# The last expert's down weights in idle up buffers, a rebuilt routing chain and a rebuilt end in a one-core decoder block

## The reference

```python
xn = rms_norm(h, norm_ffn)
logits = xn @ w_router + b_router
top_logit, top_e = lax.top_k(logits, 4)
top_w = softmax(top_logit)
# for each expert e, over the tokens that chose it:
hb = xn[tok] @ w1[e] + b1[e]                       # 1024 -> 2048
ob = clamped_swiglu(hb) @ w2[e] + b2[e]            # 1024 -> 1024
h = h + sum over the four experts of top_w * ob
out = rms_norm(h, norm_final)[:, 16:]
```

## Time and profile before

| | |
|---|---|
| three runs | 1355.83, 1360.45, 1358.1 us, median 1358.1 |
| profiled execution | 1358.35 us, its span 1356.6 us, mean granted clock 0.997 |
| PE busy | 1304.2 us (96%) |
| DVE, ACT, POOL busy | 459.3 (34%), 320.4 (24%), 66.7 (5%) |
| DMA | 461.85 MB, mean 340 GB/s |
| chain that ended last | PE 61%, DMA 29%, issue 4%, POOL 3%, DVE 2%, ACT 1% |

### The profile page before, as it was taken

The page is one execution under the profiler, slowest core; times in us unless marked ns, Lnnn a source line. Parts: engine busy times, 40 slices in busy tenths (PEclk is TensorE's granted clock), DMA queues, the critical chain, the costliest instruction groups (busy, mean ns, idle before and its releaser), DMA issues.

```text
span 1356.6 us, 17927 instructions
## 1 busy us (share of the span) xinstructions
PE 1304.2 (96%) x7105; PEld 638.0 (47%) x7105; DVE 459.3 (34%) x1129; ACT 320.4 (24%) x649; POOL 66.7 (5%) x74
## 2 busy tenths in 40 slices
PE   7999999999999999999999999999999999999995
PEld 5858888899974333333333322333333333333331
DVE  4838889988534211112111211111121111211111
ACT  3636767755411111011101101100110010111011
POOL 0000004422103000000000000000000000000000
PEclk9999999999999999999999999999999999999998
DMA  6431334244878999999999999999999999999994
GB/s 238 148 124 64 125 125 168 107 162 187 337 289 323 422 403 426 429 428 430 427 430 427 429 429 428 429 427 430 428 429 429 428 386 424 431 427 429 428 426 164
DMA packets 33763, 461.85 MB, mean 340 GB/s; under 512 B 3808, under 2 KB 3808, under 8 KB 5552
## 3 DMA queue, kind: packets, MB, share of 16 engines
q1 hardware_dynamic: 33424, 460.63, 81.5%
q10 hardware_dynamic: 288, 0.52, 0.1%
HBM read 460.09 MB, written 1.05 MB: 340 GB/s over the span
## 4 chain that ended last, share of the span: by engine, by line
PE 61%; DMA 29%; issue 4%; POOL 3%; DVE 2%; ACT 1%; SPq 0%; POOLq 0%; DVEq 0%; ACTq 0%
PE bank L1348 58%; DMA ring<-wts_dram 29%; POOL work L517 1%; POOL work L514 1%; PE bank L1690 1%; PE bank L1696 1%; DMA ring<-slabs_dram 1%; DVE split L913 0%; PE bank L1712 0%; PE bank L1479 0%; DVE work L847 0%; DVE work L846 0%; DVE work L845 0%; ACT split L559 0%; PE bank L1499 0%
## 5 line engine op out<-in xcount | busy, mean ns | idle before, releaser
L1348 PE MATMUL bank<-ring,work 128*64 128x512 f32 (+5 forms) x2248 | 541.7, 592 | 29.1 <-DMA ring<-wts_dram 28.1
L1348 PE MATMUL bank<-work 128*64 128x512 f32 (+8 forms) x2216 | 434.0, 546 | 3.2 <-DVE work L1267 1.0
L1348 PEld LDWEIGHTS bank<-ring,work 128*64 128x64 f32 (+2 forms) x2248 | 179.1, 142 | 340.4 <-issue 292.9
L1348 PEld LDWEIGHTS bank<-work 128*64 128x64 f32 (+4 forms) x2216 | 146.5, 143 | 258.8 <-issue 246.8
L1348 PE MATMUL bank<-hn_hi,split 128*128 128x256 f32 (+1 forms) x896 | 173.0, 288 | 1.4 <-DVE split L913 1.3
L1296 DVE COPY work<-bank 128x256 f32<-128x256 f32 x31 | 13.2, 425 | 473.8 <-PE bank L1712 473.8
L1348 PEld LDWEIGHTS bank<-hn_hi,split 128*128 128x128 f32 x896 | 141.4, 189 | 3.4 <-issue 1.9
L1348 PE MATMUL bank<-hn_lo,split 128*128 128x256 f32 (+1 forms) x448 | 127.2, 284 | 0.0
L1271 DVE TENSOR_SCALAR work<-bank 128x512 f32<-128x512 f32 x32 | 22.1, 692 | 273.4 <-PE bank L1348 273.4
L913 DVE TENSOR_TENSOR split<-ring,split 128x1024 fp32r<-128x1024 f32 x80 | 100.0, 1253 | 27.1 <-ACT split L559 26.8
L756 ACT ACTIVATE work<-bank 128x512 f32<-128x512 f32 x32 | 19.1, 598 | 328.3 <-PE bank L1348 324.2
(11 more groups left out here) (247 smaller groups left out, 899.9 us busy)
## 6 DMA issues: line engine op xcount, KB each, us to landing
ring<-wts_dram SPq DMA_DIRECT2D x127, 2048.0 KB, 24.2
work<-wts_dram SPq DMA_DIRECT2D x64, 2048.0 KB, 25.3
ring<-slabs_dram SPq DMA_DIRECT2D x23, 2048.0 KB, 7.5
ring<-slabs_dram SPq DMA_DIRECT2D x2, 1152.0 KB, 5.2
work<-wts_dram SPq DMA_DIRECT2D x2, 1024.0 KB, 19.8
work<-x_dram SPq DMA_DIRECT2D x3, 512.0 KB, 11.5
ring<-slabs_dram SPq DMA_DIRECT2D x1, 1536.0 KB, 12.0
ring<-slabs_dram SPq DMA_DIRECT2D x1, 1280.0 KB, 8.7
```

The source lines that it names most:

```text
L1348: return pe.matmul(o, lhsT, rhs, start=start, stop=stop)
```

## The change

Three parts, which touch one another only through the order of the work.

The last expert's down weights. Up buffers 0 and 1 of the even set take them (expert 30, the last even one, has used them after the second and the fourth k step of its up), the second in parts of 2048, 1024 and 1024 columns with a semaphore each. In SyncE's list they stand behind the second half of expert 30's.

```diff
             load_down(E - 2, E - 2)
-            load_down(E - 1, E - 1)
+            sp.wait_ge(up_used, (E - 2) * (W1_UNITS - 1) + 1)
+            sp.dma_start(w1_sb[0], unit_of(E - 1, W1_UNITS)).then_inc(w1_in[0], 16)
+            sp.wait_ge(up_used, (E - 2) * (W1_UNITS - 1) + 2)
+            for at, n, arrival in ((0, 2048, w1_in[1]), (2048, 1024, extra_in[0]), (3072, 1024, extra_in[1])):
+                sp.dma_start(w1_sb[1][:, at:at + n], unit_of(E - 1, W1_UNITS + 1)[:, at:at + n]).then_inc(arrival, 16)
...
+                if final:
+                    halves = [w1_sb[0][:, 0:UNIT // 2], w1_sb[0][:, UNIT // 2:UNIT], w1_sb[1][:, 0:UNIT // 2], w1_sb[1][:, UNIT // 2:UNIT]]
...
-                    if between is not None and k == 4:
+                    if between is not None and k == (2 if to == 4 else 4):
                         between()
```

```diff
-                link(d.max_index(idx[:, 8 * b:8 * b + 8], mx8[:, b, :], lg[:, b, :]))
-                link(d.tensor_copy(idxf[:, b, :], idx[:, 8 * b:8 * b + 8]))
-                link(d.tensor_tensor(chosen[:, b, :, :], iota_e[:, :].unsqueeze(1).to_broadcast([P, TOPK, E]),
-                                     idxf[:, b, 0:TOPK].unsqueeze(2).to_broadcast([P, TOPK, E]), ALU.is_equal))
-                d.tensor_reduce(mask[:, b, :], chosen[:, b, :, :].rearrange("p j e -> p e j"), AX.X, ALU.add).then_inc(mask_ready, 1)
+                link(d.memset(mx8[:, b, TOPK:8], -NEG))
+                link(d.match_replace(out=rest[:, b, :], in_to_replace=mx8[:, b, :], in_values=lg[:, b, :], imm_value=NEG))
+                d.tensor_scalar(mask[:, b, :], rest[:, b, :], NEG, None, ALU.is_equal).then_inc(mask_ready, 1)
...
+            a.activation(root, ssh4[:, 1, 1:2], ACT.Sqrt, scale=1.0 / D, bias=ssh[:, 1:2]).then_inc(root_ready, 1)
             xn_copy(1, 1)
...
+            def gather_first():
+                pe.wait_ge(hot_ready, 1)
+                for half, done in ((0, low_gathered), (1, gather_done)):
+                    for j in range(4):
+                        k = 4 * half + j
+                        for b in range(2):
+                            last = mm(bank[7 - half][:, j * SLOTS:(j + 1) * SLOTS], xn[:, b, k * P:(k + 1) * P], hot[:, b, :], b == 0, b == 1)
+                    last.then_inc(done, 1)
```

```diff
-            for b, n in ((1, 0), (1, 1), (0, 0)):
...
-            link(d.tensor_tensor(ssh[:, :], ssh4[:, :, 0], ssh4[:, :, 1], ALU.add))
-            rstd(rsh, ssh, D, EPS, rsh_ready)
+            d.tensor_copy(h2_copy, bank[1][:, :]).then_inc(h2_copied, 1)
+            d.wait_ge(h2_copied, 1)
+            d.tensor_tensor_reduce(out=hsq_end[:, 0, 512:D], in0=h2_copy, in1=bank[1][:, :], scale=1.0, scalar=0.0,
+                                   op0=ALU.mult, op1=ALU.add, accum_out=ssh4[:, 0, 1:2]).then_inc(h2_dve_squared, 1)
+            d.wait_ge(h2_squared, 1)
+            d.tensor_tensor(fin[:, 0, 0:512], bank[0][:, :], nfin[0][:, :], ALU.mult).then_inc(h2_scaled, 1)
...
+            link(d.reciprocal(y, root2))
+            link(d.tensor_tensor(tmp, y, y, ALU.mult))
+            link(d.scalar_tensor_tensor(tmp, ms2, -0.5, tmp, ALU.mult, ALU.mult))
+            d.scalar_tensor_tensor(y, tmp, 1.5, y, ALU.add, ALU.mult).then_inc(rsh_ready, 1)
```

More of the change, by code:

```diff
@@ L464, in _ @@
             with sp.If(cm > SLOTS):
+                sp.wait_ge(down_done, E)
                 with sp.Fori(1, SEQ // SLOTS) as r:
@@ L750, in _ @@
             top_weights(0)
+            a.activation(root, ones[:, 0:1], ACT.Sqrt).then_inc(root_table, 1)
             square_half(1, 1)
+            a.wait_ge(root_table, 1)
+            a.wait_ge(h1_squared, 4)
+            a.wait_ge(half_ready, 2)
+            a.activation(root, ssh4[:, 1, 1:2], ACT.Sqrt, scale=1.0 / D, bias=ssh[:, 1:2]).then_inc(root_ready, 1)
             xn_copy(1, 1)
@@ L789, in step @@
                     ob_of(t)
-                gathered(t0 + 1)
-                gatheredT(t0 + 1)
+                if r is FIRST:
+                    for half, done, ready in ((0, low_gathered, xgT_low_ready), (1, gather_done, xgT_ready)):
+                        cols = slice(half * SLOTS, (half + 1) * SLOTS)
+                        a.wait_ge(done, 1)
+                        a.activation(xgT[:, :, cols], bank[7 - half][:, 0:4 * SLOTS].rearrange("p (j t) -> p j t", j=4), ACT.Copy).then_inc(ready, 1)
+                else:
+                    gathered(t0 + 1)
+                    gatheredT(t0 + 1)
                 gathered(t0 + 2)
@@ L1738, in up, with down @@
                 last.then_inc(up_done, 1)
-            def down(t, to=6, actT=actT, between=None, first=None):
+            def down(t, to=6, actT=actT, between=None, first=None, later=False, final=False):
                 halves = [w2_sb[0][:, 0:UNIT // 2], w2_sb[0][:, UNIT // 2:UNIT], w2_sb[1][:, 0:UNIT // 2], w2_sb[1][:, UNIT // 2:UNIT]]
@@ L1785, in step @@
                     up_bias(t + 1)
-                    up(t + 1, pair, odd, between)
+                    up(t + 1, pair, odd, between, later=r is not FIRST)
                     if gathers:
@@ L1791, in step @@
                     if gathers:
-                        down(t, first=first)
+                        down(t, first=first, later=r is not FIRST)
                     else:
                         pe.wait_ge(scat_ready, t + 1)
-                        down(t, between=lambda: last_transposes(t + 1))
+                        down(t, between=lambda: last_transposes(t + 1), later=r is not FIRST)
                 def first_between(k):
+                    if r is FIRST and k == 4:
+                        counts()
+                    if r is FIRST and k == 2:
+                        pe.wait_ge(bias_in, 64)
+                        up_bias(t0, False)
                     if k == 6:
@@ L1829, in expert_round @@
                 if r is FIRST:
+                    pe.wait_ge(count_ready, 1)
                     cm.append(pe.value_load(cmax_i[0:1, 0:1], min_val=0, max_val=SEQ))
                 pe.wait_ge(up_read, t0 + E)
-                down(t0 + E - 1, 4, actT_last, lambda: scatter(t0 + E - 2))
+                down(t0 + E - 1, 4, actT_last, lambda: scatter(t0 + E - 2), later=r is not FIRST, final=r is FIRST)
+                pe.wait_ge(scat_ready, t0 + E)
+                scatter_last(t0 + E - 1)
             FIRST = 0
-            pe.wait_ge(xn_scaled, 2)
+            pe.wait_ge(xn_ready, 4)
             cm = []
```

210 lines of the change are left out of this document (123 added, 87 removed).

## The result

The changed kernel takes 1351.44 us (median of 5 runs, 1350.9 to 1353.01), the kernel before 1358.1 (5 runs, the three above and two more, 1355.83 to 1360.45): a ratio of 0.995, with an interval from 0.9937 to 0.9962. It is faster by 0.4 to 0.6%. The prediction was 1350.6. Its profiled execution is the one of 1351.44 us; its span is 1349.6 us, against 1356.6 before, 7.0 less.

A forecast was written before the change was run, and what follows sets the result against it. First experts were taken as bound by TensorE, later ones by the weight stream at 428 GB/s. Gains of 1.2 + 4.1 + 2.2 = 7.5 us took the median from 1358.1 to 1350.6 us, range 1347.9 to 1354.6.

The forecast's parts named there:

- Routing: Routing chain to the end of up(0): earlier masks and gather, less bias and counts inside up(0); 1.2 us gained.
- The last down weights: Last expert's down: early loads into free up buffers shorten TensorE's wait and keep the clock up; 4.1 us gained.
- The end: Final norm after the last scatter: quarters signalled separately, work shared, shorter root chain; 2.2 us gained.
- Rival A: Gather and end: gather costs 0.165 us per row, VectorE's square is held; gain 4.6 us, 1353.5 us; chance 0.18.
- Rival B: Last down loads: each lands 2 us late, routing gain lost in the stream; 1354.5 us; chance 0.13.
- Rival C: Load queue: transfers share bandwidth, so early loads delay expert 30's second half; slower, 1364.2 us; chance 0.05.

The follow-up runs named there:

- e5: The changed kernel with the old first gather and the up bias ahead of up(0) again: 1351.65 us.
- e9: The changed kernel run again, unaltered: 1351.46 us.
- e10: The changed kernel with expert 30's scatter products behind four rows of the last down instead of two: 1351.9 us.
- e3: Only the routing chain of the change, with the loads and the end of the kernel before: 1357.77 us, ratio to before 0.9995.
- e7: The changed kernel with the last expert's early down loads issued ahead of expert 30's down loads, not behind: 1362.52 us, ratio to before 1.0025.
- e1: The changed kernel with the last expert's down loads and expert 30's scatter as before: 1355.92 us, ratio to before 0.9982.
- e2: The changed kernel with the end of the kernel before: 1354.07 us, ratio to before 0.9968.
- e4: The changed kernel with expert 25's first up unit issued ahead of expert 23's down loads: 1350.25 us, ratio to before 0.994.

## Why the prediction was right

The time was 0.8 us off, and its three mechanisms are those that the runs show. All three sizes were too large, by 1.4 us together (7.5 predicted, 6.1 in the rows), and 0.9 us that were not in it made up for most of that; the closeness of the number is in that part luck.

- **Routing, +1.2 predicted, +0.55 to the second gather.** The steps up to the gather hold: it starts 13.48 us after entry, before 14.39, which is the 0.91 that the prediction had from 430.11 to 429.2. Then two terms are mis-sized. The gather's rows are 0.115 us apart, not 0.107: 3.68 to up(0), not 3.4 (-0.28). And bias and counts inside up(0) were put at 1.5; they cost 1.02 + 0.56, and the three pieces of up(0) take 3.59, 3.58 and 3.49 us, 10.66, where the unbroken 48 rows took 10.35: 0.31 for the seams, 1.89 in all. e5 shows that the new gather is a loss on TensorE: with the old one the second gather starts 0.63 us sooner. The counts and the bias took their full time inside up(0), where nothing hid them; the gain is the waits of 0.54 and 0.92 us that went. The third, 0.69, went too, but e5 has it back and is ahead all the same.
- **The last down weights, +4.1 predicted, +3.76.** The order of landings was right: 4.9 us between units, 2.5 for the half, and a wait of 1.36 (1.3 predicted). The clock stayed up. The missing 0.3: down(31) took 9.16 us to its last row, not 9.0, the last scatter waits 0.79, not 0.70, and the second wait at down(30) is 0.02 longer.
- **The end, +2.2 predicted, +1.82.** The last product came at S + 6.13, not 5.95 (rsh at S + 4.69, not 4.6), and the two transfers behind it took 0.2 longer than before to the end of the span. The square was not held: VectorE's L1372 took 0.69 us, like the copy ahead of it, all but its first 0.04 us beside GpSimd's L541 (1.27 us). The Trainium skill (SBUF — State Buffer, section "SBUF: two separate sides") ties the lock to VectorE instructions with two SBUF inputs; this one has an input in PSUM and the trace agrees.
- **What was not in the sum.** 0.33 us of a sooner entry, which is chance, and 0.54 between the second gather and down(30). The first load for expert 2 goes out at 436.25 because up(0) starts 2.44 us sooner, but most of that is given back: by 79 us after entry the stream is 0.75 us ahead of the kernel before (7.42 us short of 428 GB/s against 8.17, counted as at e5), of which 0.55 is what the second gather has won. So the sooner first load explains at most 0.2 of the 0.54. Where the rest comes from stays open; one execution against another can make it: other profiles with the same order there have from 903.93 (e9) to 904.67 us (e10) from entry to down(30), and of the kernel before there is one profile.
- **Rival A** had 0.165 per row and a held square: 0.115 and not held. **Rival B** had landings 2 us late: they were 1.4 sooner than predicted, at the predicted spacing; nor is its second half, a front lost in the stream, what the rows show, since down(30) starts 1.09 us sooner after entry (905.47, now 904.38) and in e3 1.96. **Rival C** is refuted by the rows after, where the second half of down(30) starts 4.80 us behind the first with four more loads in the queue, and by e7: put first in the queue, the early loads do cost what their bytes take (10.1 us), put last they cost nothing. The Trainium skill (DMA: Bandwidth & Descriptors, section "Queues, rings and completion order") says that each DMA engine consumes the descriptors of a ring in ring order, and the landings of e7 agree.

The parts by medians (4.5, 2.6, 0.65) sum to 7.8, more than the 7.0 of the whole (1358.42 to 1351.44), in part because a version without the early loads also pays for a low-clock stretch that varies (e1), and e2 for a later entry.

## What to carry to other kernels

Where a stream of weights ends in a wait for a buffer, look for buffers that earlier consumers have left, and put those loads behind the ones wanted first: the wrong order costs more (11.1 us in e7) than the buffers bring. Split only the transfer that is waited for. A gain on TensorE or on the stream counts only up to where the other one takes over, so price each refilled pause by the waits that it can remove, not by its bytes, and look whether it only moves (e4).

## What had not been expected

The same program enters the routing stage 1.6 us apart from one execution to another, and this is decided in the first 25 us. TensorE's first 32 rows with weights, in the profiles of the changed kernel and of e1, whose code is the same up to there:

```profile
12.01 10.36 PE L1395 MATMUL bank<-ring,work 128*128 128x320 f32 x32 [0.32 <-DMA ring<-slabs_dram]
```

```profile
12.19 11.83 PE L1390 MATMUL bank<-ring,work 128*128 128x320 f32 x32 [0.34 <-DMA ring<-slabs_dram]
```

They take 10.36 and 11.83 us at the full granted clock, and the entries are 415.39 and 416.97: the difference of 1.5 stays to the end of the stage. What sets it was not tried. In kernels with the same tail a later entry mostly goes with a later S (415.39: 1339.53; 415.65: 1339.34; 416.47: 1340.58), so two profiles are to be compared from a common mark, not from zero.

After a wait of about 3.5 us (TensorE idle) the 16 rows that follow took 5.35, 6.41 and 6.62 us in three kernels with the same order there; after 11.28 us they took 5.74, after 1.4 us 3.65. The price of the low clock is not a constant of the wait. It is half the time for which the rows run at it. By stretches of 1 us, the granted clock is 0.50 with rows running for 3.4 us in the kernel before (it falls only at about 1333.8, when the rows have started again), 6.0 in e1, 5.6 in e3 and 4.2 in e7; half of that is 1.7, 3.0, 2.8 and 2.1 us, and the 16 rows took 1.70, 2.97, 2.76 and 2.09 us more than 3.65.
